# MoE down weights: second half used by PE in fp32, and a weight ring of twelve slots instead of six

## The reference

```python
def swiglu(x, wg, wu, wd):
    return (jax.nn.silu(x @ wg) * (x @ wu)) @ wd

def step(acc, inp):                                   # of routed_experts
    tok, wt, e = inp
    y = swiglu(x_pad[tok], w_gate[e], w_up[e], w_down[e]).astype(F32) * wt[:, None]
    return acc.at[tok].add(y), None
```

## Time and profile before

| | us |
|---|---|
| median of 3 runs | 2554.88 |
| the three runs | 2554.88, 2545.16, 2558.5 |
| the profiled execution | 2554.33 |
| its span, first to last instruction | 2552.6 |
| busy in the span: PE, DVE, ACT, POOL | 2218.9, 1807.0, 1370.9, 797.9 |
| mean granted clock of TensorE, share of full | 0.941 |

### The profile page before, as it was taken

How to read it: one execution, slowest core, us unless ns; L and a number is a source line. 1 busy time by engine, 2 the same in 40 slices (tenths; PEclk the granted TensorE clock), 3 DMA queues, 4 the chain that set the end, 5 groups by cost and what they waited for, 6 DMA issues and landing times. The chain is left out here.

```text
span 2552.6 us, 37034 instructions
## 1 busy us (share of the span) xinstructions
PE 2218.9 (87%) x10633; PEld 1735.9 (68%) x10633; DVE 1807.0 (71%) x2559; ACT 1370.9 (54%) x2066; POOL 797.9 (31%) x467
## 2 busy tenths in 40 slices
PE   8989788879889999999998399998889998999992
PEld 6867667768567777777776265576677776777772
DVE  3759555535479999999997222433788998999994
ACT  3332211221358888878887122312478877888872
POOL 0000332320035555455554000000154544554451
PEclk9999898999799999999999599797999999999996
DMA  5221000000289999999997411013699999999993
GB/s 182 100 66 45 10 1 1 1 18 34 85 313 347 344 353 352 346 341 341 348 347 258 162 42 50 1 38 116 243 344 339 355 353 338 350 345 340 337 327 98
DMA packets 177845, 536.69 MB, mean 210 GB/s; under 512 B 25856, under 2 KB 55520, under 8 KB 177632
## 3 DMA queue, kind: packets, MB, share of 16 engines
q1 hardware_dynamic: 148720, 461.69, 50.0%
q0 software_dynamic: 25248, 69.25, 10.8%
q10 hardware_dynamic: 3792, 4.65, 0.5%
HBM read 501.56 MB, written 54.07 MB: 218 GB/s over the span
## 5 line engine op out<-in xcount | busy, mean ns | idle before, releaser
L1233 DVE TENSOR_TENSOR gu_l<-ring,gu_h 128x1024 fp32r<-128x1024 f32 x512 | 802.8, 1605 | 22.1 <-ACT gu_h L1119 11.1
L1119 ACT CAST gu_h<-ring 128x1024 fp32r<-128x1024 f32 x512 | 520.7, 1067 | 25.2 <-PE bank L1061 16.9
L1360 POOL TENSOR_TENSOR down_l<-ring,down_h 128x1024 fp32r<-128x1024 f32 x130 | 316.5, 2435 | 475.0 <-ACT down_h L1127 471.5
L1059 PE MATMUL bank<-gu_h,xgT_l 128*128 128x512 f32 x1024 | 412.6, 403 | 0.0
L1061 PE MATMUL bank<-gu_h,xgT_h 128*128 128x512 f32 x1024 | 401.3, 392 | 0.0
L1060 PE MATMUL bank<-gu_l,xgT_h 128*128 128x512 f32 x1024 | 400.6, 391 | 0.0
L1127 ACT CAST down_h<-ring 128x1024 fp32r<-128x1024 f32 x260 | 259.4, 1045 | 210.6 <-PE bank L1090 200.2
L1389 POOL DMA_INDIRECT moe_sum<-y,out_idx x128 | 257.3, 2010 | 201.1 <-issue 201.1
L1371 POOL DMA_INDIRECT xg<-h_rows,list_idx x128 | 130.7, 1021 | 582.2 <-DVE slot_w L1180 388.9
L1088 PE MATMUL bank<-down_h,hmT_l 128*128 128x512 f32 x544 | 224.9, 413 | 16.8 <-POOL down_l L1360 14.1
L1061 PEld LDWEIGHTS bank<-gu_h,xgT_h 128*128 128x128 f32 x1024 | 192.9, 188 | 42.2
(11 more groups left out here) (298 smaller groups left out, 3582.2 us busy)
## 6 DMA issues: line engine op xcount, KB each, us to landing
ring<-in_moe_w_gate SPq DMA_DIRECT2D x256, 512.0 KB, 7.2
ring<-in_moe_w_up SPq DMA_DIRECT2D x256, 512.0 KB, 9.5
ring<-in_moe_w_down SPq DMA_DIRECT2D x256, 512.0 KB, 6.3
ring<-in_a_w_in SPq DMA_DIRECT2D x32, 512.0 KB, 5.0
ring<-in_a_w_out SPq DMA_DIRECT2D x8, 512.0 KB, 4.1
h_rows<-y SPq DMA_DIRECT2D x8, 512.0 KB, 2.6
moe_sum<-y ACTq DMA_DIRECT2D x8, 512.0 KB, 6.7
resid<-moe_sum SPq DMA_DIRECT2D x8, 512.0 KB, 6.8
```

Of the source, the lines that this page charges most:

```text
L1059: nc.tensor.matmul(out, lhsT=xl, rhs=wh, start=k == 0, stop=False)
L1119: nc.scalar.copy(gu_h[:, c, :, :], gate_up_cols(gate_slot, c * CH // 2, CH // 2)).then_inc(gu_hi.sem, 1)
L1233: nc.vector.tensor_tensor(gu_l[:, c, :, :], gate_up_cols(gate_slot, c * CH // 2, CH // 2), gu_h[:, c, :, :].bitcast(F32), ALU.subtract).th ...
L1360: nc.gpsimd.tensor_tensor(down_l[:, 1, :], ring[:, down_slot, CH:2 * CH], down_h[:, 1, :].bitcast(F32), ALU.subtract).then_inc(down_lo.sem, 1)
```

## The change

The ring gets twelve slots, and the buffers `hT` (slots 8 and 9), `resid` (10 and 11), `z_gate` and `v_all` (6 and 7) become views of it. All loads outside the experts still go round slots 0 to 5. Expert e uses the slots of `EXPERT_SLOTS[e % 4]`, so the ring is four experts deep. `slot_free` says what frees the slot of a unit: for the first use of slots 8 and 9 the end of the shared expert's gate and up, of slots 10 and 11 `sum_done` at 4, of slots 6 and 7 nothing, later the use by the unit before. A down unit is now free when PE has used it (`down_ready`).

The second half of down is no longer split: ACT casts one half (one cast, not two), DVE makes its low part, `pool_down_lo` is gone, and PE multiplies the other half straight from the ring in fp32, by a plain copy `hmT_f` of the hidden values. So `pe_down` has six products of fp32r and two of fp32 (not twelve of fp32r). The hidden values are copied by ACT in two instructions of 128x128 (not one of 128x256), and DVE makes a low part of 128x128 (not 128x256).

```diff
--- before.py
+++ after.py
+SLOTS_IN_RING = 12
+EXPERT_SLOTS = ((0, 1, 2), (6, 7, 8), (3, 4, 5), (9, 10, 11))
...
-        ring = sb("ring", [P, RING, UNIT])
-        resid = sb("resid", [P, TT, D])
-        hT = sb("hT", [P, KD, T])
+        ring = sb("ring", [P, SLOTS_IN_RING, UNIT])
+        hT = ring[:, 8:10, :].rearrange("p a (k t) -> p (a k) t", t=T)
+        resid = ring[:, 10:12, :].rearrange("p a (b d) -> p (a b) d", d=D)
...
+        place = {}
+        in_slot = [[] for _ in range(SLOTS_IN_RING)]
+
+        def add_unit(view, width, used, value, slot):
+
+            n = len(units)
+            units[n] = (view, width, used, value)
+            place[n] = (slot, len(in_slot[slot]), in_slot[slot][-1] if in_slot[slot] else None)
+            in_slot[slot].append(n)
+            return n
+
+        turn = [0]
+
+        def next_slot():
+            turn[0] += 1
+            return (turn[0] - 1) % RING
...
-            units[n + 2] = (flat(a["moe_ws_down"][layer]), None, down_lo, down)
-            n += 3
-            UNIT_EXPERT[layer] = n
+                add_unit((gate[:, half], up[:, half]), None, gu_ready, gu_shared, next_slot())
+            add_unit(flat(a["moe_ws_down"][layer]), None, down_ready, down, next_slot())
+            UNIT_EXPERT[layer] = len(units)
+            for slot, used, value in ((8, gu_ready, gu_shared), (9, gu_ready, gu_shared), (10, sum_done, TT * (layer + 1)), (11, sum_done, TT * (layer + 1))):
+                in_slot[slot].append((used, value))
             for e in range(E):
-                units[n] = (None, None, gu_lo, gu + CH_GU * e + CH_GU // 2)
-                units[n + 1] = (None, None, gu_lo, gu + CH_GU * (e + 1))
-                units[n + 2] = (None, None, down_lo, down + CH_DOWN * (e + 1))
...
+                slots = EXPERT_SLOTS[e % 4]
+                add_unit(None, None, gu_lo, gu + CH_GU * e + CH_GU // 2, slots[0])
+                add_unit(None, None, gu_lo, gu + CH_GU * (e + 1), slots[1])
+                add_unit(None, None, down_ready, down + e + 1, slots[2])
...
+        def slot_of(n):
+            return place[n][0]
+
+        def slot_free(n):
+
+            before = place[n][2]
+            if before is None or isinstance(before, tuple):
+                return before
+            return units[before][2:]
+
+        def loaded(n):
+
+            slot, turn_no, _ = place[n]
+            done = sum(1 for m in in_slot[slot][:turn_no] if not isinstance(m, tuple))
+            return slot_loaded[slot].sem, LOADED * (done + 1)
...
-        z_gate = sb("z_gate", [P, TT, D], scope=gdn)
+        z_gate = ring[:, 6:8, :].rearrange("p a (b d) -> p (a b) d", d=D)
...
+                    arrivals, value = loaded(n0 + j)
+                    eng.wait_ge(arrivals, value + LOADED * i)
+                return slot_of(n0), slot_of(n0 + 2), arrived
...
             def pe_down(pe, r, i, shared=False):
                 m = r if shared else TT + r
                 s = 0 if shared else r + 1
-                pe.wait_ge(down_lo.sem, down_lo.base + CH_DOWN * (s + 1) + 4 * CH_DOWN * i)
+                _, down_slot, arrived = item_units(r, i, shared)
+                pe.wait_ge(down_lo.sem, down_lo.base + s + 1 + 4 * i)
+                if not shared or r == 0:
+                    arrived(pe, 2)
                 pe.wait_ge(hmT_copied.sem, hmT_copied.base + m + 1 + 4 * i)
                 if 1 <= m <= TT:
                     pe.wait_ge(sum_done.sem, sum_done.base + m)
                 elif m > TT:
                     pe.wait_ge(y_done.sem, y_done.base + r + 4 * i)
+                xh, xl, xf = hmT_h[:, m % 2, :], hmT_l[:, m % 2, :], hmT_f[:, m % 2, :]
                 for half in range(2):
-                    for j in range(2):
-                        out = bank[6 + half][:, :]
-                        xh, xl = hmT_h[:, m % 2, j, :], hmT_l[:, m % 2, j, :]
-                        wh, wl = down_h[:, j, half * 512:half * 512 + 512], down_l[:, j, half * 512:half * 512 + 512]
-                        nc.tensor.matmul(out, lhsT=xl, rhs=wh, start=j == 0, stop=False)
-                        nc.tensor.matmul(out, lhsT=xh, rhs=wl, start=False, stop=False)
-                        last = nc.tensor.matmul(out, lhsT=xh, rhs=wh, start=False, stop=j == 1)
+                    out, c = bank[6 + half][:, :], slice(half * 512, half * 512 + 512)
+                    nc.tensor.matmul(out, lhsT=xl, rhs=down_h[:, c], start=True, stop=False)
+                    nc.tensor.matmul(out, lhsT=xh, rhs=down_l[:, c], start=False, stop=False)
+                    nc.tensor.matmul(out, lhsT=xh, rhs=down_h[:, c], start=False, stop=False)
+                    last = nc.tensor.matmul(out, lhsT=xf, rhs=ring[:, down_slot, CH + half * 512:CH + half * 512 + 512], start=False, stop=True)
                 last.then_inc(down_ready.sem, 1)
...
-                for c in range(CH_DOWN):
-                    nc.scalar.copy(down_h[:, c, :], ring[:, down_slot, c * CH:(c + 1) * CH]).then_inc(down_hi.sem, 1)
+                nc.scalar.copy(down_h[:, :], ring[:, down_slot, 0:CH]).then_inc(down_hi.sem, 1)
...
-                nc.scalar.copy(hmT_h[:, m % 2, :, :], heads(bank[4][:, 0:2 * P])).then_inc(hmT_hi.sem, 1)
+                nc.scalar.copy(hmT_h[:, m % 2, :], bank[4][:, 0:P])
+                nc.scalar.copy(hmT_f[:, m % 2, :], bank[4][:, P:2 * P]).then_inc(hmT_hi.sem, 1)
...
-                nc.vector.tensor_tensor(hmT_l[:, m % 2, :, :], heads(bank[4][:, 0:2 * P]), hmT_h[:, m % 2, :, :].bitcast(F32), ALU.subtract).then_inc(hmT_copied.sem, 1)
+                nc.vector.tensor_tensor(hmT_l[:, m % 2, :], bank[4][:, 0:P], hmT_h[:, m % 2, :].bitcast(F32), ALU.subtract).then_inc(hmT_copied.sem, 1)
...
-            def pool_down_lo(pool, r, i, shared=False):
-
-                _, down_slot, _ = item_units(r, i, shared)
-                s = 0 if shared else r + 1
-                pool.wait_ge(down_hi.sem, down_hi.base + CH_DOWN * (s + 1) + 4 * CH_DOWN * i)
-                nc.gpsimd.tensor_tensor(down_l[:, 1, :], ring[:, down_slot, CH:2 * CH], down_h[:, 1, :].bitcast(F32), ALU.subtract).then_inc(down_lo.sem, 1)
...
                 if not last or r + 3 < E:
                     pool_gather(pool, r + 3, i)
-                pool_down_lo(pool, r, i)
                 if r >= 1:
                     pool_scatter(pool, r - 1, i)
...
                     def load_unit(r, i, j):
                         n = U + 3 * r + j
-                        _, _, used, value = units[n - RING]
-                        sp.wait_ge(used.sem, value + 4 * (CH_GU if used is gu_lo else CH_DOWN) * i)
+                        if slot_free(n):
+                            used, value = slot_free(n)
+                            sp.wait_ge(used.sem, value + 4 * (CH_GU if j < 2 else 1) * i)
                         for h in range(2):
 
                             w, c0 = (weights[h], j * HALF) if j < 2 else (weights[2], h * HALF)
-                            sp.dma_start(ring[:, n % RING, h * HALF:(h + 1) * HALF], w[bass.ds(r + 4 * i, 1), :, c0:c0 + HALF].rearrange("e p c -> (e p) c")).then_inc(slot_loaded[n % RING].sem, 16)
+                            sp.dma_start(ring[:, slot_of(n), h * HALF:(h + 1) * HALF], w[bass.ds(r + 4 * i, 1), :, c0:c0 + HALF].rearrange("e p c -> (e p) c")).then_inc(slot_loaded[slot_of(n)].sem, 16)
...
                     load_gate_up(0, 0)
-                    for r in range(2):
+                    for r in range(4):
                         load_gate_up(r + 1, 0)
                         load_down(r, 0)
-                    with sp.Fori(0, (E - 4) // 4) as i:
-                        for r in range(2, 6):
+                    with sp.Fori(0, LOOP) as i:
+                        for r in range(4, 8):
                             load_gate_up(r + 1, i)
                             load_down(r, i)
-                    load_gate_up(E - 1, 0)
-                    load_down(E - 2, 0)
+                    for r in range(E - 4, E - 1):
+                        load_gate_up(r + 1, 0)
+                        load_down(r, 0)
                     load_down(E - 1, 0)
...
-        v_all = sb("v_all", [P, TT, D], scope=att)
+        v_all = ring[:, 6:8, :].rearrange("p a (b d) -> p (a b) d", d=D)
```

More of the change, by code:

```diff
@@ L63 @@
 CH_GU = 4
-CH_DOWN = 2
 CH = 1024
@@ L139, in heads @@
             return ap.rearrange("p (h q) -> p h q", q=P)
-        slot_loaded = [sem(f"slot_loaded{i}") for i in range(RING)]
+        slot_loaded = [sem(f"slot_loaded{i}") for i in range(SLOTS_IN_RING)]
         small_in = sem("small_in")
@@ L169, in build @@
         uq_ready = sem("uq_ready")
+        sum_done = sem("sum_done")
         def rows_kp(w, c0, width):
@@ L205, in tail_units @@
                 half = slice(j * HALF, (j + 1) * HALF)
-                units[n + j] = ((gate[:, half], up[:, half]), None, gu_ready, gu_shared)
-            units[n + 2] = (flat(a["moe_ws_down"][layer]), None, down_lo, down)
-            n += 3
-            UNIT_EXPERT[layer] = n
```

(28 more changed lines are left out.)

60 lines of the change are left out of this document (24 added, 36 removed).

## The result

The changed kernel took **2480.97 us** in the median (2478.74 to 2494.24, 4 runs); the kernel before, run beside it, 2554.9. The ratio is 0.974, with a 95% interval of 0.970 to 0.978. Run again later beside four other kernels it took 2488.7 (ratio 0.975, 0.973 to 0.977).

A forecast was written before the change was run, and what follows sets the result against it. The prediction took full DMA engines at 344 GB/s as the bound. Layer start, end and lead summed to 2 x (1.7 - 1.2 - 5.3) = -9.6 us from 2554.3, giving 2544.7 (said 2545), range 2503 to 2576.

The forecast's parts named there:

- What bounds the kernel now: MoE expert steps: full DMA engines at 344 GB/s taken as the bound, 10.66 us a step in layer 0.
- Queues the same bytes behind full engines: Expert loads: a deeper ring removes SP's waits for slots but only queues the same bytes; no gain in steady steps.
- POOL's subtraction: Expert steps: removing it returns 1.87 us of DVE's time a step, costed at nothing beside the DMA engines.
- PE's down: Expert steps: six fp32r products go, two fp32 come, +0.34 us, covered; PE-paced steps 9.91 become 10.25; down 2.9 to 3.2.
- rival 1: Expert steps: DVE's chain, not DMA engines, was the bound; PE then paces at 10.25, 2503 us; chance 0.32 with middle cases.
- Start of a layer: Start of each MoE layer: nine units issued early, the tenth waits for `sum_done`; +1.7 us a layer.
- End and lead: Each MoE layer: removing idle channel at the end, -1.2 us on average; using up the loads' lead, -5.3 us.
- Tail: Last experts: a shorter wait for POOL's last `down_l`, some 1.4 us, against 1.4 for slower down products; nil.
- middle case: Expert steps: engines get a little fuller because more is queued; a step of 10.45, -27 us, 2527; within 0.32.
- Rival 2: Expert steps: scatters and gathered rows come late behind deep load queues; 27 us more, 2572 us; chance 0.15.
- Rival 3: Whole change: it does not do what it says; the kernel stays within some us of 2554; chance 0.05.
- The rule of 425 GB/s: Expert loads: a core streaming alone reaches about 425 GB/s, so 3.67 MB takes 8.6 us and the channel is no bound.

The follow-up runs named there:

- experiment 1: Changed kernel with loads held to two experts ahead instead of four: 2536.8 us, ratio 0.997 to the kernel before.
- experiment 6: Changed kernel with loads held to two experts ahead and two of the three gate and up products left out: 2521.15 us, ratio 0.988.
- experiment 5: Changed kernel with two of the three products of gate and up left out on PE: 2484.54 us.
- experiment 9: Changed kernel with DVE's copies of the row lists moved ahead of the gate and up subtractions: 2485.92 us.
- experiment 10: Changed kernel with the second DMA of each down unit cut to 16 columns and DVE's row-list copies moved earlier: 2445.48 us.
- experiment 3: Changed kernel with POOL's subtraction put back, 832 columns into a tile nothing reads: 2510.61 us, ratio 0.985.
- experiment 11: Changed kernel with gate and up of expert 4 issued ahead of the unit waiting for `sum_done`: 2480.23 us, again 2472.09; with early row-list copies 2472.69.
- experiment 7: Changed kernel with each DMA of a down unit half as wide, 0.52 MB of an expert's weights unloaded: 2522.03 us.
- experiment 8: Changed kernel with the second DMA of each down unit cut to 16 columns, 0.52 MB of an expert's weights unloaded: 2578.07 us.
- experiment 12: Changed kernel with the two DMAs of a down unit split by partitions instead of columns, rows of 8192 bytes: 3152.54 us, ratio 1.238.

## Why the prediction was wrong
**What bounds the kernel now: wrong, and this is the step that failed.** "This is the picture of DMA engines that are full, and I take them as the bound." What the runs show in its place is four limits that lie close together. They are DVE's chain with POOL's lock, about 10.66 us a step in the kernel before; loads held to two experts ahead, 10.5 to 10.7 (experiments 1 and 6, with the later release of down slots); loads with a full queue, 10.14 (experiments 5, 9 and 10); PE, 9.68. That the kernel before sat on the first is read from its waits; no run takes the lock alone out of it. The change without its depth brought 0.3% (experiment 1), and with its depth but POOL's subtraction back 1.5% (experiment 3). The whole change brought 2.6%, more than the two together, and the third limit now binds.

The row that could have told it was quoted in the prediction itself: the last `w_up` lay there 5.3 us before ACT read it. Loads that bind are not ready early. The list of waits says the same for layer 0: ACT waits for no load, PE in each step for `hm`. The falling behind of the earlier trace rows was real but never reached ACT.

**"Queues the same bytes behind full engines": the same failure in the sum.** With the engines taken as the bound, all that DVE got back was put at nothing in the steady steps, and so was the deeper ring. A share of 1.00 was read as full, and 344 GB/s as what full engines move. With a full queue the same engines moved 363 at a share of 1.02. A step moves about 3.68 to 3.69 MB at either: 10.66 x 345 and 10.14 x 364. The term put at nothing was worth 0.53 us in 122 steps, 64 of the 75.7 us of span. The stretches with a filled queue in the kernel before pointed that way, though they are short. From 1435 to 1450, where loads for the attention ahead of layer 1's experts run:

```profile
1435.00:1450.00 15.00, 7.08 (x31) 5.88 (x31) 12.11 (x18) 4.03 (x10) 0.00 (x0) 0.50 1.05 382
```

**POOL's subtraction:** the size was right, 1220 ns for `gu_l` after the earlier trace rows, as the lock rule of the Trainium skill's "SBUF — State Buffer" has it, and experiment 3 brings it back to 1615. Its cost was put at nothing and is 22 to 30 us with deep loads by the medians (15 to 18 in the steps).

**PE's down:** right. The two ends after, answering to the earlier trace rows:

```profile
777.20 0.39 PE L1117 MATMUL bank<-down_h,hmT_l 128*128 128x512 f32 x1
...
780.30 0.38 PE L1099 MATMUL bank<-const,hm 128*128 128x128 f32 x2
```

3.10 us, inside the 2.9 to 3.2 named, and 0.27 more than twelve products at 0.236 (0.34 was forecast). But the PE-paced step of 10.25 was wrong: 9.91, the first step before, already held a wait for `hm`, and the pace is 9.68. Had rival 1 used that, its 2503 would have been 2434, and the truth would have been inside the range.

**Start of a layer:** the mechanism is there. SP's timeline, the ninth unit and the tenth, which waits for `sum_done`:

```profile
706.20 0.62 SPq L1453 DMA_DIRECT2D ring<-in_moe_w_gate  x1
706.86 0.46 SPq L1453 DMA_DIRECT2D ring<-in_moe_w_up  x1
732.58 0.33 SPq L1453 DMA_DIRECT2D ring<-in_moe_w_gate  x1
```

Its +1.7 us can't be read off against the kernel before: the silu of expert 1 comes 1.3 us earlier, as loads don't bind yet there. That the standing queue does cost something later shows in experiment 11, which fills it and saves 3.0 to 6.3 us a layer. **End and lead:** the lead is used up as forecast (ACT now waits for the last loads of layer 0); as loads bind on the average of the steps, it can't be told apart from them. **Tail:** nil, as forecast (0.3 us).

**Rival 1** was right that DVE's chain bound, and its middle case ("engines that get a little fuller because more is queued") named the second mechanism, at a third of its size. **Rival 2**'s mechanism exists in other kernels, but not as priced: with deeper queues the scatter landed earlier (7.8 for 9.1), and it was the gather, with emptier queues, that came late in experiments 7 and 8. **Rival 3** did not happen.

**The rule of 425 GB/s** ("HBM Reference" of the Trainium skill): no long stretch came near. With a full queue the kernels whose loads bound moved 358 to 365 GB/s, scatters and gathers among it.

## What to carry to other kernels
Ask of a bound that it shows as a wait: if no consumer waits for a load, the DMA engines are not the bound, whatever their busy share. Tell a full queue from a fed one by the issuing engine: waiting for slots with short issues means room, issues of 2 to 5 us mean full; only the rate of the latter says what the channel can move. And where several limits lie within a few per cent, price a change against the next one that stays, since two removed together can bring more than the sum of what each brings alone.

## What was unexpected of the hardware
- The busy share of the DMA engines says little of throughput. It was 1.00 at 345 GB/s, 1.02 at 364, and 1.02 at 242 when down units went into half of the partitions at a time. From the queue's rows, engine time per MB of loads (share x 16 x 590 us / MB) was 41.7 us in the changed kernel and 66.5 in experiment 12. Whether half the partitions or the longer rows did it was not separated.
- Removing 17% of a step's load bytes made the kernel 41 and 89 us slower (the second against the changed kernel beside it), with PE waiting for gathered rows 32 and 45 us in 590. With DVE's list copy some 5 us earlier the latter kernel took 40 us less than the changed one with the same early copy. That the gathers land later because SP's loads come in bursts is a guess from the timeline; why they should, against a queue that is always full, stays open.
- The granted clock of one 40 us stretch of attention, with PE busy throughout, was 0.57 to 0.95 in executions of nearly the same code, and the time between the layers went with it, from 452 to 435 us.
